# Part of the output product moved into the recurrence chain of an RWKV-7 mixer, and the work around its group norm reordered

## What is computed

```python
y = _wkv7_scan(rh, wh, kh, vh, -kk, kk * ah)          # 12 heads of 64 channels, 256 tokens
mean = jnp.mean(y, axis=-1, keepdims=True)
var = jnp.mean(jnp.square(y - mean), axis=-1, keepdims=True)
y = ((y - mean) * lax.rsqrt(var + GN_EPS)).reshape(B, S, MIX_WIDTH)
y = y * lnx_w + lnx_b
bonus = jnp.sum(rh * kh * r_k, axis=-1, keepdims=True) * vh
out = (y + bonus.reshape(B, S, MIX_WIDTH)) * g         # 768 channels
...
cross = _mem_attention(q_mem, mn, w_kv[i])             # the four memory heads, 256 channels
x = x + jnp.concatenate([mix, cross], axis=-1) @ w_o[i]
x = x + _swiglu(_rmsnorm(x, norm2[i]), w_ffn_in[i], w_ffn_out[i])
```

## Time and profile before

| | |
|---|---|
| time, median of 3 runs | 1285.11 us (1283.18 to 1285.41) |
| time of the profiled execution | 1282.11 us |
| span of the profiled execution | 1280.3 us |
| PE busy | 1204.6 us (94%) |
| DVE busy | 759.6 us (59%) |
| ACT busy | 595.4 us (47%) |
| mean granted PE clock | 0.966 of full speed |

### The profile page before, as it was taken

The page is one execution under the profiler, slowest core; times in us unless marked ns, Lnnn a source line. Parts: engine busy times, 40 slices in busy tenths (PEclk is TensorE's granted clock), DMA queues, the critical chain, the costliest instruction groups (busy, mean ns, idle before and its releaser), DMA issues.

```text
span 1280.3 us, 24099 instructions
## 1 busy us (share of the span) xinstructions
PE 1204.6 (94%) x10320; PEld 1109.7 (87%) x10320; DVE 759.6 (59%) x1289; ACT 595.4 (47%) x1003; POOL 38.8 (3%) x44
## 2 busy tenths in 40 slices
PE   5999989999999998799799999999989988999997
PEld 4999878999988877798489999889988986999985
DVE  5555646666646677634566666465744575666644
ACT  4666545444435642232344444354328655444433
POOL 0000000000000102331000000000000000000000
PEclk9999989999999979899799999999989998999999
DMA  9822124867555431000259665537544343676651
GB/s 271 237 87 83 67 67 116 224 183 197 183 188 154 152 99 66 2 4 3 67 149 262 188 177 196 197 104 226 179 151 124 108 161 103 168 195 185 180 195 66
DMA packets 222693, 184.50 MB, mean 144 GB/s; under 512 B 19394, under 2 KB 208080, under 8 KB 222460
## 3 DMA queue, kind: packets, MB, share of 16 engines
q1 hardware_dynamic: 221386, 181.50, 47.6%
q10 hardware_dynamic: 1202, 1.47, 0.3%
HBM read 181.90 MB, written 1.05 MB: 143 GB/s over the span
## 4 chain that ended last, share of the span: by engine, by line
PE 83%; DVE 10%; ACT 4%; issue 1%; SPq 1%; DMA 1%; DVEq 0%; ACTq 0%
PE bank L776 23%; PE bank L777 22%; PE bank L778 22%; DVE w_lo L2027 2%; PE bank L1055 2%; PE bank L1273 1%; ACT w_hi L1580 1%; PE bank L1039 1%; PE bank L1249 1%; DMA ring<-in_nsa_w_in 1%; PE bank L1257 1%; PE bank L919 1%; SPq L713 1%; PE bank L923 1%; DVE act_lo L1997 1%
## 5 line engine op out<-in xcount | busy, mean ns | idle before, releaser
L2027 DVE TENSOR_TENSOR w_lo<-ring,w_hi 128x1024 fp32r<-128x1024 f32 x326 | 383.1, 1216 | 264.8 <-ACT w_hi L1580 264.6
L1580 ACT ACTIVATE w_hi<-ring 128x1024 fp32r<-128x1024 f32 x326 | 323.4, 1041 | 425.9 <-PE bank L778 407.4
L776 PE MATMUL bank<-act_hi,w_hi 128*128 128x256 f32 (+1 forms) x1512 | 428.0, 283 | 6.1 <-issue 3.4
L777 PE MATMUL bank<-act_lo,w_hi 128*128 128x256 f32 (+1 forms) x1512 | 424.6, 281 | 0.0
L778 PE MATMUL bank<-act_hi,w_lo 128*128 128x256 f32 (+1 forms) x1512 | 424.1, 280 | 0.0
L776 PEld LDWEIGHTS bank<-act_hi,w_hi 128*128 128x128 f32 (+1 forms) x1512 | 284.7, 188 | 10.7 <-issue 6.7
L777 PEld LDWEIGHTS bank<-act_lo,w_hi 128*128 128x128 f32 (+1 forms) x1512 | 284.6, 188 | 0.3
L778 PEld LDWEIGHTS bank<-act_hi,w_lo 128*128 128x128 f32 (+1 forms) x1512 | 283.9, 188 | 0.3
L776 PE MATMUL bank<-w_hi,act_hi 128*128 128x256 f32 (+1 forms) x448 | 141.0, 315 | 8.5 <-DVE act_lo L2503 4.2
L777 PE MATMUL bank<-w_lo,act_hi 128*128 128x256 f32 (+1 forms) x448 | 138.9, 310 | 0.0
L778 PE MATMUL bank<-w_hi,act_lo 128*128 128x256 f32 (+1 forms) x448 | 138.5, 309 | 0.0
(11 more groups left out here) (312 smaller groups left out, 1292.1 us busy)
## 6 DMA issues: line engine op xcount, KB each, us to landing
ring<-in_w_ffn_in SPq DMA_DIRECT2D x88, 512.0 KB, 5.2
ring<-in_w_in SPq DMA_DIRECT2D x28, 1024.0 KB, 5.3
ring<-in_w_ffn_out SPq DMA_DIRECT2D x22, 1024.0 KB, 4.9
ring<-in_rw_w_in SPq DMA_DIRECT2D x11, 1024.0 KB, 5.3
ring<-in_w_gate SPq DMA_DIRECT2D x22, 512.0 KB, 4.0
ring<-in_w_up SPq DMA_DIRECT2D x22, 512.0 KB, 5.2
ring<-in_w_down SPq DMA_DIRECT2D x11, 1024.0 KB, 4.9
ring<-in_w_o SPq DMA_DIRECT2D x8, 1024.0 KB, 4.9
```

What stands on the lines that cost most here:

```text
L776: pe.matmul(o, ahl[0], bhl[0], start=first, stop=False)
L777: pe.matmul(o, ahl[0], bhl[1], start=False, stop=False)
L1580: act.activation(w_hi[:, (m % SPLITS) * SLOT + lo:(m % SPLITS) * SLOT + hi], ring[:, r * SLOT + lo:r * SLOT + hi], copy).then_inc(tick(own ...
L2027: dve.tensor_tensor(w_lo[:, c], ring[:, r * SLOT + lo:r * SLOT + hi], w_hi[:, c].bitcast(F32), ALU.subtract).then_inc(tick(own, "lo_ready" ...
```

## The change

The change has these parts.

- The output product begins with `wo1_3`. Its first 12 matmuls are put, three at a time (`cross_product`, steps 0 to 3), behind the last merge, `late2`, `z3` and `late3`; steps 4, 5, 6 stand between `gm` and `gv`, and step 7 between `gv` and `gr`. The other three units follow, of which `wo1_2` is now the last. The product goes to banks 4 to 7, and the transposes behind it to banks 0 to 3.
- The weights of `wo1_3` are split during the second pair's merge s = 16. To make this possible the scores of the first pair and of the second lie in different split buffers (`sc_parts`), and POOL's masks lie in `act_hi`.
- The gate and the norm's weight and bias are applied ahead: DVE makes (bonus + bias) x gate in the merges of the first pair (before, POOL added the bias ahead of the merges), and ACT makes gate x weight in the merges of the second pair. After the root DVE multiplies `y` with that product (`weigh`), for the first third ahead of the reciprocal.
- Per third there are now two DVE operations in place of four, and the low part of a third is made after the next third's, not after all three.
- ACT loads the table of the square root ahead of reading out `late3`. The split of a second output slot by ACT comes behind the root.

```diff
+    CROSS_AFTER = {("late", 2): 1, ("z", 3): 2, ("late", 3): 3}
...
+    for j in range(3):
+        unit(f"gm_{j}")
+    unit("gv")
+    out_row(3)
+    for j in range(3):
+        unit(f"gr_{j}")
+    for j in range(3):
+        out_row(j)
...
-        pool.wait_ge(*evacuated("bs_2"))
-        for i in range(NT):
-            ins = pool.tensor_scalar(bonus[:, i, :], bonus[:, i, :], V("rw_lnx_b", i), None, ALU.add)
...
+        def cross_product(step):
+
+            qt, a, half = step // 4, step // 2 % 2, step % 2
+            if step == 0:
+                pe.wait_ge(*evacuated("crT"))
+                piece("wo1_3", 1)
+            if a == 0:
+                b, before = uses["wo1_3"][2 * qt + half]
+                pe.wait_ge(bank_free[b], before)
+            k = 6 + a
+            ins = product(bank_of("wo1_3", 2 * qt + half)[:, :], [v[:, k, qt * P:(qt + 1) * P] for v in fm],
+                          [v[:, a, half * 512:(half + 1) * 512] for v in split("wo1_3", 2)], a == 0, False)
+            if step == 7:
+                ins.then_inc(unit_done, 1)
...
+            cross_product(0)
             for hop, c in LAST_HOPS:
                 hops[hop](c)
+                if (hop, c) in CROSS_AFTER:
+                    cross_product(CROSS_AFTER[hop, c])
...
+        for step in (4, 5, 6):
+            cross_product(step)
         head_sums("gv", zt, "squares_ready", 1)
+        cross_product(7)
         pe.wait_ge(sem("rstd_ready"), 1)
         head_spread("gr", narrow)
...
# ACT, in the merges of the second pair
+                if pr:
+                    li = MERGES.index(s)
+                    for i in range(li, NT if s == 32 else li + 1):
+                        act.wait_ge(sem("bonus_ready"), i + 1)
+                        act.activation(g_fm[:, i, :], g_fm[:, i, :], copy, scale=V("rw_lnx_w", i)).then_inc(tick(own, "gate_scaled"), 1)
+                if pr and s == 16:
+                    split_to(split_no["wo1_3"] + 1)
         for hop, c in LAST_HOPS:
+            if (hop, c) == ("late", 3):
+                act.wait_ge(*last(own))
+                act.activation(bn[:, 1:2], bn[:, 0:1], ACT.Sqrt).then_inc(tick(own), 1)
             act_hop(hop, c)
...
# DVE, in the merges
+                if pr == 0:
+                    li = MERGES.index(s)
+                    for i in range(li, NT if s == 32 else li + 1):
+                        dve.scalar_tensor_tensor(out=bonus[:, i, :], in0=bonus[:, i, :], scalar=V("rw_lnx_b", i), in1=g_fm[:, i, :],
+                                                 op0=ALU.add, op1=ALU.mult).then_inc(tick(own, "bonus_ready"), 1)
+                    dve.wait_ge(*last(own))
                 if pr and ("t", s) in CHAIN_SLOTS:
                     dve_hop(*CHAIN_SLOTS["t", s])
+                if pr and s == 16:
+                    split_to(split_no["wo1_3"] + 1)
...
# DVE, after gv
+        weigh(0)
+        dve.wait_ge(sem("gstd_ready"), 1)
+        dve.reciprocal(narrow[0:H, :], narrow[0:H, :]).then_inc(tick(own, "rstd_ready"), 1)
+        weigh(1), weigh(2)
+        dve.wait_ge(*last(own))
+        for j in range(3):
+            dve.wait_ge(*filled(f"gr_{j}"))
+            ts = slice(2 * j, 2 * j + 2)
+            dve.tensor_tensor(flat(y_fm[:, ts, :]), bank_of(f"gr_{j}")[:, :], flat(y_fm[:, ts, :]), ALU.mult).then_inc(freed(own, f"gr_{j}"), 1)
+            dve.wait_ge(*last(own))
+            dve.tensor_tensor(mix_fm[:, ts, :], y_fm[:, ts, :], bonus[:, ts, :], ALU.add).then_inc(tick(own, "mix1_ready"), 1)
+            if j:
+                low_mix(j - 1)
+        low_mix(2)
```

More of the change, by code:

```diff
@@ L166, in build @@
     x_res = place("x_res", QT * D)
+    ACT_HI = fixed_at[0]
     act_hi = place("act_hi", KT * S, dtype=F32R)
@@ L290, in build, with score_parts, sc @@
     arena_at[0] = 0
-    sc = [take(H * 4 * CH).rearrange("p (u b t) -> p u b t", u=H, b=4) for _ in range(2)]
-    ems = [take(4 * CH).rearrange("p (u t) -> p u t", u=4) for _ in range(3)]
-    cms = [take(4 * CH).rearrange("p (u t) -> p u t", u=4) for _ in range(3)]
-    assert arena_at[0] <= FREE
+    EARLY_SLOT = 0
+    def score_parts(b):
+        return [arena[:, o:o + n * 4 * CH].rearrange("p (u b t) -> p u b t", u=n, b=4)
+                for o, n in ((W_HI + b * SLOT, 8), (W_LO + b * SLOT, 4))]
+    sc_parts = [score_parts(EARLY_SLOT), score_parts(1 - EARLY_SLOT)]
+    def sc(pr, us):
+        if isinstance(us, int):
+            us = slice(us, us + 1)
+        part, first = (sc_parts[pr][0], 0) if us.start < 8 else (sc_parts[pr][1], 8)
+        assert us.stop - first <= (8 if first == 0 else 4)
+        return part[:, us.start - first:us.stop - first]
+    ems = [arena[:, W_LO + (1 - EARLY_SLOT) * SLOT + (4 + gi) * 4 * CH:W_LO + (1 - EARLY_SLOT) * SLOT + (5 + gi) * 4 * CH]
+           .rearrange("p (u t) -> p u t", u=4) for gi in range(3)]
+    cms = place("cms", 3 * 4 * CH, ACT_HI - SHARED).rearrange("p (g u t) -> p g u t", g=3, u=4)
+    cms = [cms[:, gi] for gi in range(3)]
     arena_at[0] = FREE
@@ L839, in tile_product @@
                 for half in range(2):
-                    ins = product(bank_of(f"{tag}0", 2 * qt + half)[:, :], [v[:, k, qt * P:(qt + 1) * P] for v in act],
-                                  [v[:, a, half * 512:(half + 1) * 512] for v in w], k == 0, k == 2 * n - 1)
+                    ins = product(bank_of(f"{tag}{first}", 2 * qt + half)[:, :], [v[:, k, qt * P:(qt + 1) * P] for v in act],
+                                  [v[:, a, half * 512:(half + 1) * 512] for v in w], k == 2 * first, k == 2 * final + 1)
                 return ins
-            if j < n - 1:
+            if j != final:
                 for a in range(2):
@@ L1840, in _ @@
             act.activation(fm[0][:, 2 * j:2 * j + 2, :], mix_fm[:, 2 * j:2 * j + 2, :], copy).then_inc(tick(own, "mix1_hi"), 1)
-        rows_ahead("wo1")
-        act.wait_ge(*evacuated("wo1_0", 1))
+        ahead("wo1_0"), ahead("wo1_1")
+        act.wait_ge(*evacuated("wo1_3", 1))
         squares(4, x_tm)
-        from_banks([(fm, lambda k: ("norm2", 8 + k))])
-        ahead("wo1_3")
+        from_banks([(fm, lambda k: ("norm2", 8 + k))], 0)
+        ahead("wo1_2")
         root(4)
@@ L2504, in _ @@
                               ALU.subtract).then_inc(tick(own, "mix1_lo"), 1)
-        split_to(split_no["wo1_1"] + 1)
-        rows_ahead("wo1")
-        residual("wo1_0", "wo1_3")
-        from_banks([(fm, lambda k: ("norm2", 8 + k))])
+        weigh(0)
[3 more added lines that the diff above has]
+        dve.wait_ge(*last(own))
+        for j in range(3):
+            dve.wait_ge(*filled(f"gr_{j}"))
+            ts = slice(2 * j, 2 * j + 2)
+            dve.tensor_tensor(flat(y_fm[:, ts, :]), bank_of(f"gr_{j}")[:, :], flat(y_fm[:, ts, :]), ALU.mult).then_inc(freed(own, f"gr_{j}"), 1)
+            dve.wait_ge(*last(own))
+            dve.tensor_tensor(mix_fm[:, ts, :], y_fm[:, ts, :], bonus[:, ts, :], ALU.add).then_inc(tick(own, "mix1_ready"), 1)
+            if j:
+                low_mix(j - 1)
+        low_mix(2)
+        ahead("wo1_3"), ahead("wo1_0"), ahead("wo1_1")
+        residual("wo1_3", "wo1_2")
+        from_banks([(fm, lambda k: ("norm2", 8 + k))], 0)
         mean_square(4, x_tm)
-        ahead("wo1_3")
+        ahead("wo1_2")
         inverse(4)
```

59 lines of the change are left out of this document (23 added, 36 removed).

## The result

The changed kernel takes 1271.49 us (median of 12 runs, 1267.52 to 1274.82), the kernel before 1280.76 us (12 runs, 1271.95 to 1289.72): a ratio of 0.9936, 95% interval 0.9915 to 0.9958. By the ratio that is 8.2 us less, by the two medians 9.3 us. In another session, with other runs of both kernels, the ratio was 0.9901 (0.9877 to 0.9924), 12.7 us less by the ratio and 11.2 by the medians (1282.15 and 1270.96 us). The forecast ratio was 1277.1 / 1285.11 = 0.9938.

The account below looks back on a forecast made before the run. PE's waits, some 11.2 us, were to take 24 product matmuls: -1.6 (chain) + 2.8 (earlier product) + 5.6 (fewer matmuls) + 1.2 (clock) = 8.0 us gained, so 1277.1 us, range 1275.0 to 1279.0.

Parts of the forecast that it names:

- The level: Whole kernel: the gain was set against the median of three runs, 1285.11 us, 3.0 us above the profiled execution.
- Chain: Up to the end of `late3`: added work on ACT, DVE and PE loses 0.4 + 1.0 + 0.2 = 1.6 us.
- the low part: Between the additions of s = 16 and 32: DVE's two low parts of `wo1_3` delay the chain by 1.0 us.
- The gate multiplication: Behind the readout of the first chunk's output: ACT's added 128x256 multiplication delays the next readout, losing 0.4 us.
- The groups: Four groups of three product matmuls in the chain, 0.7 us each, mostly fill PE's idle time and cost 0.2 us.
- The table load: Ahead of the chain's last readout: the 1.28 us load fits in ACT's idle 2.26 us and costs nothing.
- the further drain: At the table load: about 1.38 us more by the skill, making the last readout some 0.5 us late; not counted.
- `gm` to `gr`: Three product groups delay `gv` by 1.9 us; with `weigh(0)` ahead of the reciprocal, `gr` comes 0.95 us later.
- `gr` to the product: Fewer DVE operations, with low parts made earlier: 3.5 us from the first third; PE begins the product 2.8 us earlier.
- The product: 24 of 96 matmuls leave it, 5.6 us; 8 or fewer at the low clock, not 14, give 1.2 us more.
- The wait ahead of `gr`: PE's wait there for the reciprocal shrinks from 4.2 to about 2.4 us.
- the new stall: Near 598 us: DVE's low parts idle PE 1 us longer, bringing half clock into the chain; 8.3 us slower, chance 0.06.

Follow-up runs that it names:

- the product back: Changed kernel with all eight groups of the `wo1_3` product moved back behind the wait for the first low part; ratio to the kernel before 1.0014.
- all behind `gv`: Changed kernel with all eight product groups placed behind `gv`, none in the chain; ratio to the kernel before 0.9982.
- the kernel before with both delays: Kernel before plus an ACT copy of 128x256 and, between two merges' additions, two DVE products of 128x1024, all into unused memory; ratio to it 1.0056.
- the copy on ACT: Kernel before plus one ACT copy of 128x256 of the gate into unused memory, behind the first chunk's output readout; ratio to it 1.0023.
- the norm alone: Changed kernel with the whole product back at its end and the low part of `wo1_3` made behind the last merge's additions; ratio to the kernel before 1.0002.

## Why the prediction was right or wrong

**The level was wrong.** The step is the last of the sum: "The three runs have a median of 1285.11 us, 3.0 us above that execution, so on the scale of the median 1277.1 us". Twelve runs of the kernel before have a median of 1280.76 us, 4.35 us lower, and single runs reach from 1271.95 to 1289.72; four other groups of 17 to 23 runs have medians of 1280.4 to 1282.15 us. Taken from the twelve, the forecast gain of 8.0 us gives 1272.8 us. So of the 5.6 us between 1277.1 and 1271.49, 4.35 are the level and 1.3 the gain, which is 9.3 us by the medians. The range allowed "2 us of what three runs spread", where twelve spread over 17.8 us.

**The gain was right in size, and nearly so term by term.** Chain: 1.6 us lost by forecast, 1.8 measured (74.1 to 75.9 us on the means of five and three profiles). In it the low part is 0.9 us (10.50 against 9.61 between the first matmuls of `z2` and `u2`), where I had 1.0. The gate multiplication is 0.4, as forecast: the first matmul of `z1` stands 3.6 us behind that of `late0` in place of 3.2. The groups cost some 0.5 us together, not 0.2: 0.1 for the first, and 13.28 us in place of 12.92 from `u2` to `gm`. The table load cost nothing, and the further drain of which I wrote by "ScalarE: Activation LUTs" (What ACT_TABLE_LOAD costs) in the Trainium skill does not show: the load took 1.28 us, the one-element root started at its end, and the last readout stood where PE's end put it.
`gm` to `gr`: 0.95 us longer by forecast, 0.7 measured, because the reciprocal started 8.61 us behind `gm` (615.22 less 606.61) and not 8.85. `gr` to the product: 5.0 us by forecast, 4.64 measured, because the two multiplications in a row took 1.21 and not 1.4 us, and the product began 3.40 us behind the first third and not 3.55. The product: 6.8 us shorter by forecast (5.6 and 1.2), 6.3 measured. In it the clock was low for 4.35 us, some 10 matmuls, where I had 8. The wait ahead of `gr` was 2.0 us for 2.4. That the sum comes out so near is in part luck: each term is off by up to 0.5 us, and the errors nearly cancel.

**What the mechanism lacked** is what the groups in the chain do for the clock. I had entered them as filling idle time and given the fall of the clock there a chance of 0.06, as a price of the new stall. The runs speak for two things, a stall that brings the fall nearer and groups that keep it away. With the stall and no groups: falls in all three profiles that have it (the product back, all behind `gv`, the kernel before with both delays), stretches of 127.9 to 142.9 us. With four groups in the chain: none in seven profiles. With three groups and no stall one fall in two, with neither one in one of the changed chain and none in six of the kernel before's (the copy on ACT among them). The falls are counts of single profiles, most versions have one, and the edits also shift the work behind them, so the runs show how often the clock fell and not why. Taking out the four groups costs 5.2 us, of which some 3 are the clock's by the estimate above, and putting back all eight 9.5 to 10, of which 6.3 to 6.8 are. The remark in the Trainium skill's "TensorE: Matmul & The Clock Gate" (HAM oscillation), that idle gaps bring the half clock and PE kept at work avoids it, agrees with no fall in seven profiles with four groups; I had used it for the waits around `gr` only, where the clock fell in every version all the same, ahead of the product's first matmul or within 1 us behind it.

**Open.** The timed gain is 8.2 us in one session and 12.7 in another by the ratios, the stretch's 7.8. In the timed runs of the second session the mean granted clock was 0.9685 for the changed kernel and 0.9647 before, 9.7 us less at the low clock over the span ((0.9685 - 0.9647) x 2 x 1275), of which the stretch has 6.9 (13.7 to 6.8 us). I expected some executions of the kernel before to lose the clock in the hops, as its times spread over 6 to 18 us and the changed kernel's over 5 to 7; five profiles show none. Where up to 5 us of the timed gain lie is not settled. Nor is why the chain of the norm alone lost the clock where that of the kernel before did not.

## What to carry to other kernels

Read a change of a few microseconds from a stretch between two fixed instructions, in more than one profile, and take the level of "before" from many runs: here the stretch repeats within 0.6 us and the whole time within 18 us. In this serial chain of small matmuls, independent matmuls put into the short waits were worth more than their own time, since no profile with four groups lost the clock there; and delays of 1.4 us went with 11 us in one profile. Place such work where the next step waits for another engine anyway (behind `gv`, 1.9 us better up to `gr` and 1.4 in the stretch), and no more of it than that wait holds (there four groups; the fifth cost 0.6 us), and not ahead of a reduction on the path (between `gm` and `gv`, 2.1 us saved and 1.9 lost).

## What the runs showed of the hardware

The clock fell in a chain in which PE was nearly always busy by its rows. In the kernel before with both delays these are the stages around the fall:

```profile
575.00:588.00 13.00, 12.95 (x403) 1.00 0.01 4
588.00:592.80 4.80, 2.84 (x73) 1.00 0.02 3
592.80:611.20 18.40, 16.75 (x249) 0.50 0.01 2
```

Two waits for DVE, of 1.27 and 0.68 us, among matmuls of 64x64 stood in the 4.8 us ahead of it (start us, us, what, [idle before <-releaser]):

```profile
590.34 0.68 PE L1055 MATMUL bank<-tt,arena 64*64 64x64 f32 x16 [1.27 <-DVE tt L2472]
591.71 1.61 PE L1084 MATMUL bank<-arena,tt 64*64 64x64 f32 x22 [0.68 <-DVE tt L2472]
```

In the 18.4 us behind it PE was busy 16.75 us without getting the full clock back. In the product, with matmuls of 128x512, the full clock was back 3.1 to 7.6 us behind the first matmul, over all versions.
